# Two RWKV layers in a hybrid model's kernel: inverses by masked copies and transposes, the end by token halves, the first layer's mixing ahead of the norm

## The reference

```python
def rwkv7_time_mix(h, v_first, mix, w_rkv, ...):
    shifted = jnp.pad(h, ((0, 0), (1, 0), (0, 0)))[:, :-1]
    xm = h[:, :, None, :] + (shifted - h)[:, :, None, :] * mix
    r, k, v = einsum(xm[:, :, :3], w_rkv)
    logw = -softplus(-(w0 + tanh(xw @ w1) @ w2)) - 0.5      # decay
    a = sigmoid(a0 + (xa @ a1) @ a2)                        # rate
    g = sigmoid(xg @ g1) @ g2                               # gate
    # second RWKV layer: v = v + (v_first - v) * sigmoid(v0 + (xv @ v1) @ v2)
    def step(state, inp):
        sa = einsum('bhvk,bhk->bhv', state, kk_t)
        state = state * w_t - sa * (kk_t * a_t) + v_t * k_t
        return state, einsum('bhvk,bhk->bhv', state, r_t)
    y = (y - mu) * rsqrt(var + eps) * ln_w + ln_b           # per head
    y = y + sum(r * k * r_k) * v
    return (y * g) @ w_out
```

## Time and profile before

| what | value |
|---|---|
| median of 3 runs | 1935.93 us (1933.72 to 1939.68) |
| the profiled execution | 1935.0 us, its span 1932.9 us |
| TensorE matmuls busy | 1817.4 us (94%) |
| VectorE busy | 1263.3 us (65%) |
| ScalarE busy | 1029.7 us (53%) |
| GpSimd busy | 146.0 us (8%) |
| mean granted clock of TensorE | 0.974 |

### The profile page before, as it was taken

One profiled execution on the slowest core, in us unless ns is written; L12 is line 12 of the kernel. 1 busy time (PEld: TensorE's weight loads), 2 busy tenths in 40 slices (PEclk: granted clock), 3 DMA queues, 4 the chain that ended last, 5 costly groups with the idle time before them and its releaser, 6 DMA issues.

```text
span 1932.9 us, 43768 instructions
## 1 busy us (share of the span) xinstructions
PE 1817.4 (94%) x18871; PEld 1631.5 (84%) x18871; DVE 1263.3 (65%) x1783; ACT 1029.7 (53%) x1585; POOL 146.0 (8%) x106
## 2 busy tenths in 40 slices
PE   6987999999989999898999999998899999998998
PEld 5887788889979888887698888887798888887887
DVE  6875367865436675486668856876467755775764
ACT  5834455554535554354655545744465554564455
POOL 0051100000000000014000000151100000000000
PEclk9999999999989999899899999999999999998999
DMA  6420145557576655355465562320245555443441
GB/s 190 132 86 4 53 146 184 190 182 244 174 233 217 197 191 180 110 174 178 150 198 184 186 204 93 120 76 4 68 153 191 178 188 169 134 146 104 152 132 66
DMA packets 288535, 287.92 MB, mean 149 GB/s; under 512 B 15240, under 2 KB 286456, under 8 KB 288344
## 3 DMA queue, kind: packets, MB, share of 16 engines
q1 hardware_dynamic: 285048, 284.02, 45.8%
q10 hardware_dynamic: 3296, 1.11, 0.3%
HBM read 284.06 MB, written 1.05 MB: 148 GB/s over the span
## 4 chain that ended last, share of the span: by engine, by line
PE 90%; DVE 4%; issue 3%; ACT 2%; DMA 0%; POOL 0%; SPq 0%; DVEq 0%; ACTq 0%; POOLq 0%
PE ps L419 23%; PE ps L420 12%; PE ps L401 10%; PE ps L403 9%; PE ps L402 9%; PE ps L814 3%; PE ps L436 2%; PE ps L437 2%; PE ps L438 2%; PE ps L713 1%; PE ps L784 1%; PE ps L798 1%; PE ps L675 1%; PE ps L641 1%; PE ps L727 1%
## 5 line engine op out<-in xcount | busy, mean ns | idle before, releaser
L463 DVE TENSOR_TENSOR wl<-raw,wh 128x1024 fp32r<-128x1024 f32 x484 | 596.5, 1251 | 345.4 <-ACT wh L453 340.9
L453 ACT ACTIVATE wh<-raw 128x1024 fp32r<-128x1024 f32 x484 | 499.4, 1041 | 432.0 <-PE ps L420 191.2
L419 PE MATMUL ps<-HH,wh 128*128 128x512 f32 x1408 | 489.7, 391 | 0.0
L420 PE MATMUL ps<-HH,wl 128*128 128x256 f32 x1408 | 397.0, 282 | 0.0
L419 PEld LDWEIGHTS ps<-HH,wh 128*128 128x128 f32 x1408 | 264.3, 188 | 55.6 <-issue 0.4
L401 PE MATMUL ps<-HH,wh 128*128 128x256 f32 x928 | 271.4, 292 | 10.2 <-DVE HH L2498 5.5
L420 PEld LDWEIGHTS ps<-HH,wl 128*128 128x128 f32 x1408 | 266.1, 189 | 0.1
L402 PE MATMUL ps<-HH,wh 128*128 128x256 f32 x928 | 263.6, 284 | 0.0
L403 PE MATMUL ps<-HH,wl 128*128 128x256 f32 x928 | 263.3, 284 | 0.0
L401 PEld LDWEIGHTS ps<-HH,wh 128*128 128x128 f32 x928 | 179.3, 193 | 20.8 <-issue 6.6
L402 PEld LDWEIGHTS ps<-HH,wh 128*128 128x128 f32 x928 | 179.6, 193 | 1.2 <-issue 1.2
(11 more groups left out here) (323 smaller groups left out, 3119.6 us busy)
## 6 DMA issues: line engine op xcount, KB each, us to landing
raw<-in_ffn_w_gu_dram SPq DMA_DIRECT2D x88, 1024.0 KB, 5.1
raw<-in_ffn_w_down_dram SPq DMA_DIRECT2D x32, 1024.0 KB, 5.1
raw<-in_w_in_dram SPq DMA_DIRECT2D x32, 1024.0 KB, 5.4
raw<-in_rw_w_rkv_dram SPq DMA_DIRECT2D x24, 1024.0 KB, 5.3
B<-in_w_ada_dram SPq DMA_DIRECT2D x24, 1024.0 KB, 7.7
raw<-in_ds_w_in_dram SPq DMA_DIRECT2D x14, 1024.0 KB, 5.3
raw<-in_ffn_w_down_dram SPq DMA_DIRECT2D x16, 768.0 KB, 4.4
raw<-in_sb_w_qkv_dram SPq DMA_DIRECT2D x12, 1024.0 KB, 5.5
```

The costliest lines, as they stand in the source:

```text
L419: e.matmul(o[:, m, :], h_[:, k, c], x_, start=k0 + k == 0, stop=False, skip_group_check=True)
L420: i = e.matmul(o[:, m, 0:S], l_[:, k, c], x_[:, 0, :], start=False, stop=k0 + k == kt - 1, skip_group_check=True)
L453: e.activation(wh[:, u % UNITS, 0:kn * 256], raw[:, j % RAW, k0 * 256:(k0 + kn) * 256], ACT.Copy).then_inc(*up("hi"))
L463: e.tensor_tensor(wl[:, u % UNITS, 0:kn * 256], raw[:, j % RAW, k0 * 256:(k0 + kn) * 256], wh[:, u % UNITS, 0:kn * 256].bitcast(F32), ALU. ...
```

## The change

The inverse `T` starts as minus the identity (`clear`), and each level writes its off-diagonal quarter into it with `copy_predicated` under a mask `low{m}` (VectorE). The transpose of T comes no longer from a second product but from 16 transposes on TensorE a level (`turned`), copied by ScalarE. The left factor of a first product is the whole copy `At` of the gram, with no mask by level, so GpSimd's masks and the gram "bq" go. The projection blocks within the levels are split in two halves (`block_halves`) on a kept bank 0, the other tiles turn over seven banks. The grams "br" and "kr" and bTM's transposes move ahead of the product G. The end works by halves of 128 tokens: `centred(t)`, `spread(t, m)`, `weighted`, `gated`, `rest_y`; the gate multiplies before the scale, and gates 0 and 1 run earlier. In layer 0 the low-rank weights of decay and rate are mixed ahead of the normed input, with a semaphore of its own for the gate's weights; the mixing of the receptance's input moves behind the running sums, on ScalarE behind the first evacuation. The core of the diff:

```diff
+            for name, a, z, landed_ in (("rw_w1", 0, 64, s_down), ("rw_a1", 64, 128, s_down), ("rw_g1", 128, 256, s_down_g)):
+                e.dma_start(down[:, :, a:z], wview(A[name][n])[:, :, 0:z - a]).then_inc(landed_, 16)
...
+            def block_halves(m, p, g):
+                key, free = ("full", n, m, g), ("dve", ("vmix", n, g)) if n and m == 2 else ("act", ("full", n, m, g))
+                ready = [[("dve", ("xml", n, m, k // 2))] for k in range(KD)] if g == 0 else None
+                o = kept_bank(e, 0, key, free)
+                for k0, kn, u in next_units(KD):
+                    fm_unit(e, key, o, KD, k0, kn, u, parts_of(*((HH, HL), (XH, XL))[p]), ready)
+                    yield
...
+            def quarters(key, m, j, L, Rr, by):
+                os = [bank(e, (key, n, m, j, a), (by, (key, n, m, j, a))) for a in range(2)]
+                for q in range(8):
                     for b in range(2):
-                        for o, g in zip(os, pair):
-                            a = b ^ side_in(g) ^ side_out(g)
-                            i = e.matmul(o[half(b), p_ * HD:p_ * HD + HD], L[half(a), g[0], g[1], p_, :], Rr[half(a), g[0], g[1], p_, :],
+                        for a in range(2):
+                            i = e.matmul(os[a][half(b), q * HD:q * HD + HD], L[half(a), j, q, b, :], Rr[half(a), j, q, b, :],
                                          start=True, stop=True, skip_group_check=True)
-                            if p_ == 7 and b == 1:
...
+                            if q == 7 and b == 1:
+                                i.then_inc(*up("mm", (key, n, m, j, a)))
+            def turned(m, j):
+                for r in range(2):
+                    o = bank(e, ("turn", n, m, j, r), ("act", ("turn", n, m, j, r)))
+                    for q in range(4):
+                        i = e.transpose(o[:, q * P:q * P + P], BUF[6][:, (8 * j + 4 * r + q) * P:(8 * j + 4 * r + q) * P + P], ident)
+                    i.then_inc(*up("mm", ("turn", n, m, j, r)))
             def first_products(m):
-                for pair in pairs_at(m):
...
+                for j in range(2):
+                    for a in range(2):
+                        e.wait_ge(*at("act", ("bp", n, j, a)))
+                        e.wait_ge(*at("dve", ("low", n, m // 2, j, a)))
+                    quarters("xs", m, j, At, T, "dve" if m == 32 else "act")
+                for j in range(2):
+                    turned(m // 2, j)
             def second_products(m):
-                def s_in(g):
...
+                for j in range(2):
+                    for a in range(2):
+                        e.wait_ge(*at("dve" if m == 32 else "act", ("xs", n, m, j, a)))
+                        e.wait_ge(*at("act", ("turn", n, m // 2, j, a)))
+                    if m == 32:
+                        quarters("tt", m, j, Xw, Tw, "act")
+                    else:
+                        quarters("low", m, j, Tw, X1, "dve")
...
+            cur["first"] = 1
             for j in range(2):
                 gram("pb", j, Pm, Bt_)
             for j in range(2):
                 gram("bp", j, Bt_, Pm)
-            gram("bq", 1, Bt_, Pm, 1)
-            full(0, 1, 3)
-            first_products(2)
+            last_read = block_halves(0, 1, 3)
+            next(last_read)
...
+            next(last_read)
             for g in range(4):
-                full(2, 0, g)
+                first_products(LEVELS[g])
+                values = block_halves(2, 0, g)
+                next(values)
                 second_products(LEVELS[g])
-                if g < 3:
-                    first_products(LEVELS[g + 1])
+                next(values)
+            first_products(32)
             for j in range(2):
                 gram("kp", j, Kp, Pm)
+            second_products(32)
+            cur["first"] = 0
             for j in range(2):
                 pe_to_tm(e, ("pTM", n, j), Pm, j)
+            for j in range(2):
+                gram("br", j, Bt_, R_)
             e.wait_ge(*at("dve" if n else "act", ("vmix", n, 3) if n else ("full", n, 2, 3)))
             for j in range(2):
                 pe_to_tm(e, ("V", n, j), v_, j)
-            first_products(32)
             for j in range(2):
-                gram("br", j, Bt_, R_)
-            second_products(32)
+                gram("kr", j, Kp, R_)
+            for j in range(2):
+                pe_to_tm(e, ("bTM", n, j), Bt_, j)
             for j, par in groups:
                 e.wait_ge(*at("act", ("V", n, j, 1)))
...
+            def centred(t):
+                for m in range(2):
+                    if t == 0 and m == 1:
+                        cur["bank"] += 2
+                    o = bank(e, ("cen", n, t, m), ("dve", ("cen", n, t, 2 * m + 1)))
+                    e.wait_ge(*at("act", ("y", n, 2 * t + 1)))
+                    e.matmul(o[:, :], C("cent"), Y[:, 4 * m:4 * m + 4, t * P:t * P + P], start=True, stop=True,
+                             skip_group_check=True).then_inc(*up("mm", ("cen", n, t, m)))
+            def spread(t, m):
+                o = bank(e, ("var", n, t, m), ("act", ("var", n, t, m)))
+                e.wait_ge(*at("act", ("ysq", n, t, m)))
+                e.matmul(o[:, :], C("bavg"), ysq[:, 4 * m:4 * m + 4, :], start=True, stop=True,
+                         skip_group_check=True).then_inc(*up("mm", ("var", n, t, m)))
             own_values(0)
             keys_values(0, 2)
             y_values(0)
             from_state(1)
             new_state(1)
             new_y(1)
+            gate(0)
+            gate(1)
             keys_values(1, 1)
             y_values(1)
             from_state(2)
             new_state(2)
             new_y(2)
-            gate(0)
-            gate(1)
+            centred(0)
             from_state(3)
+            spread(0, 0)
+            spread(0, 1)
+            new_y(3)
             gate(2)
-            new_y(3)
+            centred(1)
+            spread(1, 0)
+            spread(1, 1)
+            cur["bank"] += 1
             gate(3)
-            Y, sq = FM(6), FM(0)
...
             pe_out_proj(e, layer, parts_of(XH, XL), [[("dve", ("yl", n, k // 2))] for k in range(KD)])
...
-            hi(e, 2 if n else 4)
-            prepare(1, HH)
+            hi(e)
+            if n:
+                prepare(1, HH)
             e.wait_ge(*at("mm", ("wa", n)))
             e.activation(lor[0:64, :], PS("wa", n)[0:64, 0:S], ACT.Tanh)
             e.activation(lor[64:128, :], PS("wa", n)[64:128, 0:S], ACT.Copy).then_inc(*up("act", ("wa", n)))
-            prepare(0, XH)
+            if n:
+                prepare(0, XH)
+            else:
+                prepare(1, HH)
+                hi(e)
             e.wait_ge(*at("mm", ("g", n)))
             e.activation(sg[:, 0, :], PS("g", n)[:, 0:S], ACT.Sigmoid).then_inc(*up("act", ("g", n)))
             for g in range(4):
...
+            if n == 0:
+                prepare(0, XH)
+                hi(e)
...
+            def clear(j):
+                e.wait_ge(*at("dve", ("rn read", n, j)))
+                e.activation(BUF[6][:, j * 1024:j * 1024 + 1024].rearrange("p (q t) -> p q t", t=HD),
+                             C("eye").unsqueeze(1).to_broadcast([P, 16, HD]), ACT.Copy, scale=-1.0).then_inc(*up("act", ("minus eye", n, j)))
             hi(e)
             evac(0, 0, R_)
             hi(e)
             evac(0, 1, R_)
+            clear(0)
+            clear(1)
             e.wait_ge(*at("mm", ("gv", n)))
             e.activation(sg[0:32, 1, :], PS("gv", n)[0:32, 0:S], ACT.Sigmoid).then_inc(*up("act", ("gv", n)))
...
+            def quarters_out(key, m, j, dst, scale=1.0):
+                for a in range(2):
+                    e.wait_ge(*at("mm", (key, n, m, j, 1)))
+                    e.activation(dst[:, j, :, a, :], q8(PS(key, n, m, j, a)[:, :]), ACT.Copy, scale=scale).then_inc(*up("act", (key, n, m, j, a)))
+            def turned(m):
+                for j in range(2):
+                    for r in range(2):
+                        copy_out(("turn", n, m, j, r), Tt[:, j, r, :])
             for j, par in groups:
...
+            e.wait_ge(*at("mm", ("gv", n)))
+            e.wait_ge(*at("dve", ("PB", n, 1)))
+            e.activation(BUF[0][:, :].rearrange("p (q t) -> p q t", t=HD), C("eye").unsqueeze(1).to_broadcast([P, 32, HD]),
+                         ACT.Copy).then_inc(*up("act", ("eye", n)))
+            evac(0, 3, R_)
             for g in range(4):
+                for j in range(2):
+                    quarters_out("xs", LEVELS[g], j, X1)
+                hi(e, 1)
+                turned(LEVELS[g] // 2)
                 hi(e, 1)
                 if n == 0:
                     evac(2, g, v_)
-                second_products(LEVELS[g])
...
             log_and_exp(e)
+            turned(16)
+            for j in range(2):
+                quarters_out("tt", 32, j, Tn, -1.0)
...
             negate_u(0)
             y_out(0)
             negate_u(1)
```

(123 more changed lines are left out.)

257 lines of the change are left out of this document (79 added, 178 removed).

## The result

The changed kernel takes 1941.95 us, median of 12 runs (1935.78 to 1948.90), against 1934.01 us of the kernel before in the same session (12 runs, 1930.53 to 1939.68). The ratio is 1.0039, 95% interval 1.0027 to 1.0051: it is slower by 0.4%. The prediction said 1921.0, in 1906 to 1940, and is wrong in sign and in range. The profiled execution took 1944.42 us, its span is 1942.3 (before: 1935.0 and 1932.9).

What follows compares the result with a forecast made beforehand. TensorE's work and waits in the two RWKV layers were taken as the bound; 1.9 + 13.3 + 1.5 + 7.4 - 6.8 - 3.4 = 13.9 us off 1935.0 gave 1921, range 1906 to 1940.

Steps and rivals of the forecast that it cites:

- list of the new kernel's waits: TensorE's work plus expected waits from gram to V transposes: 82.2 us in layer 0, 92.4 in layer 3.
- Opening, 1.9 us: Layer 0's start: TensorE begins 5.5 us earlier, ScalarE's list takes the rest, 1.9 us gained.
- Layer 0's inverses, 13.3 less 3.4 for two falls: Layer 0, gram to V: fewer waits, 95.5 to 82.2 us, 13.3 gained; two clock falls at 1.7 each taken off.
- a level of 14.25: One level of the inverses: 12.0 us of TensorE work plus a 2.25 us wait for ScalarE, without a clock fall.
- idle or slow: Layer 0's inverses before the change: 23.3 of 95.5 us in which TensorE was idle or at a lowered clock.
- Layer 3, 1.5 less 3.4 for two falls: Layer 3's inverses: 93.95 to 92.4 us, 1.5 gained; two clock falls at 1.7 each taken off.
- "waits change their name" rival: Opening and inverses: new waits eat the whole 13.9 us gain, 0.7 a level from ScalarE-VectorE turns; 1935 us, chance 0.11.
- Four of eight: Inverse levels of both layers: the 2.25 us wait makes the clock fall in four of eight, 1.7 us each, 6.8 lost.
- "fall in every level" rival: Clock falls in all eight inverse levels and at both ends, leaving 7.1 us gained; 1928 us, chance 0.17.
- Ends, 7.4 less 3.4: Ends of both layers: output projection's second unit 3.7 us earlier each, 7.4 gained; two clock falls, 3.4, taken off.
- The slower rival: VectorE's masked copies in the inverses cost from 1.2 us each; at 2.0 they give 1952 us; chance 0.12.

Runs made afterwards that it cites:

- e4: The kernel before with only the new opening of layer 0: 1934.1 us, ratio 0.9997 to the kernel before.
- e11: e7 with half a read block between the grams, constant products before the first key norm, masked copies before the value mix, erase-key turning between grams kp: 1891.6 us.
- e9: The changed kernel with 8 extra constant products on TensorE ahead of the wait in each lower level: 1928.8 us, ratio 0.9978 to the kernel before.
- e12: e7 with the weight piece that lands during the grams fetched only when the grams bp are done, both layers: 1899.6 us, ratio 0.9819 to the kernel before.
- e13: The kernel before with the weight piece that lands during the grams fetched only when the grams bp are done: 1931.8 us, ratio 0.9988.
- e1: The changed kernel with ScalarE copying the transposed banks before rounding the weight unit in each lower level: 1923.2 us, ratio 0.9937 to the kernel before.
- e6: e1 with VectorE subtracting a weight unit behind the level's masked copies instead of ahead of the decays: 1911.6 us, ratio 0.9872 to the kernel before.
- e7: e6 with ScalarE's identity copy and read-outs moved earlier and layer 3's value gates behind the last read block: 1906.8 us, ratio 0.9846 to the kernel before.
- e3: The kernel before with only the new layer ends by token halves: 1929.4 us, ratio 0.9973 to the kernel before.
- e2: The kernel before with only the new inverses, old opening and old ends: 1950.9 us, ratio 1.0090 to the kernel before.

## Why the prediction was wrong, step by step

Set beside the traces, the sum fails in two places. Up to layer 0's recurrence it had 1.9 + 13.3 - 3.4 = 11.8 us gained, and 0.6 were lost. For layer 3 it had 1.5 - 3.4, so 1.9 lost, and between layer 0's end and layer 3's recurrence 18.7 were lost. The ends, with all that follows layer 3's recurrence, gained 4.4 + 5.5 = 9.9 where 4.0 were forecast. The step that failed in both places is the list of the new kernel's waits, 82.2 us from the gram to the V transposes in layer 0 and 92.4 in layer 3. The traces have 96.0 and 109.8.

**Opening, 1.9 us: the times held, the gain did not.** Key norms ended at 64.89; predicted 64.9. But the prediction moved TensorE's start by 5.5 us and its key norm by 2 without pricing the idle time that this leaves ahead of the norm. TensorE was busy for 1.1 us of 58 to 61, the clock fell to 0.50, and the read block behind ran at 0.21 us a product instead of 0.12. The gain was gone by the gram; e4 measures 0.6 us, not to be told from zero. In e11, without the fall, the gram starts at 88.64, 1.4 us ahead of the predicted one.

**Layer 0's inverses, 13.3 less 3.4 for two falls: 82.2 us were 96.0.** Much of the mechanism was right: the rounding starts at the end of the half block, two copies behind it, 2.25 us; a level of 14.25 is 14.5 in e9. Also right: the masked copy at 0.72 us (predicted 0.69) and the subtraction at 1.2 without GpSimd, here in layer 3 (count, busy us and mean ns of one, idle before):

```profile
L456 DVE TENSOR_TENSOR wl<-raw,wh 128x1024 fp32r<-128x1024 f32 x14 | 16.9, 1221 | 50.4 <-ACT wh L446 50.4
L2330 DVE COPY_PREDICATED B<-CT,ps 128x512 f32<-128x512 int32 x20 | 13.1, 717 | 0.5 <-PE ps L812 0.5
```

The error is in the other side of the subtraction. Of the old kernel's 95.5 us the 23.3 "idle or slow" (23.5, if the list of TensorE's work is added up right, to 72.0) went in as recoverable unless a listed wait of the new kernel took their place. 2.45 of them was the unnamed stretch with 1.7 of fall behind it. The new list of waits did not hold it, and it stayed with 2.59 us; e12 and e13 show that all but 1 us of it in this layer hangs on the place of a weight transfer that both kernels have. The V transposes ended at 187.6 for the predicted 172.3: 5.8 us late at the first level (1.5 from the opening, the stretch, its fall), 5.8 more over the levels, most of it the falls (3.4 had been set down for them apart), and 3.7 in the tail, where two more unnamed stretches stand (1.23 and 1.35 us).

**Layer 3, 1.5 less 3.4 for two falls: 92.4 us were 109.8.** TensorE reached the first level at 1267.1, where the prediction's list, counted from the gram at 1245.8 (4.0 + 0.85 + 5.8 + 3.65), comes to 1260.1. These 7.0 us are the stretch of 2.79, not in the list, and the clock behind it (0.71 over 1252 to 1255, 0.50 over 1261 to 1264): both half blocks ran at up to 0.21 us a product, and the value gates took 4.49 us for 16 products (3.65 before). ScalarE's sigmoids, identity and evacuation then cost no more than the 4.0 that the list had for them. The levels took 7.4 more than forecast: 16.7 us each (roundings at 1277.69 and 1294.39) against 14.25 + 0.5, and of these 2 us a level 1.5 are the fall, since e9, without it, has 15.2. The rest fits VectorE's subtraction, which waits for a rounding, holds the value mixes, and these hold the kept bank. The last 3.0 us lie in the tail. e1 and e6, which change ScalarE's and VectorE's order alone, take 21 us of layer 3 back, waits and falls together, so that order was the cause of most of the loss. The "waits change their name" rival named the turns of ScalarE and VectorE, at 0.7 us a level; it named neither the stretch nor the falls.

**The clock: price right, count wrong.** 1.7 us a fall is confirmed by e9. Four of eight was a choice between 1.86 us (no fall) and 2.45 (fall); seven fell. The "fall in every level" rival was near in this count, not in its time (1928). The Trainium skill, "TensorE: Matmul & The Clock Gate", Part 4 (PE-mode transpose), says that the full clock does not engage for transposes. By it all eight would have fallen, one more than did, but the runs do not bear it out as the cause: e9 and e7 have the same 16 transposes a level, and their clock stays at 1.00 in all of layer 0's levels.

**Ends, 7.4 less 3.4: right within the noise.** The rounding behind the second unit, which started at 253.98, starts at 250.23:

```profile
250.23 1.06 ACT L446 ACTIVATE wh<-raw 128x1024 fp32r<-128x1024 f32 x1 [0.61 <-PE ps L391]
```

That is 46.5 us after the recurrence's first product, against 50.9 before (253.98 less 203.11, same instruction): 4.4 in layer 0. The fall forecast for this place came, inside that time:

```profile
243.00:245.00 2.00, 2.00 (x11) 0.50 1.09 378
```

So the trace has 4.4 where 3.7 less 1.7 was forecast. e3 measures 5.2 for both layers (3.1 to 7.3), which holds the forecast 4.0 and not twice 4.4; where the rest went, no run shows. The prediction's reading that TensorE had nothing to do from 240 to 246.70 before the change was not quite right: the windows from 243 to 247 have 1.75 us of work, at a clock of 0.83 and 0.50.

**The slower rival** came nearest with its sign, by the wrong mechanism: it needed masked copies of over 1.2 us, and they take 0.72. That the kernel came out slower, as this rival said, is luck.

## What to carry to other kernels

When an edit removes waits, list every idle stretch of the old kernel with its cause, and credit only those whose cause the edit removes; a stretch without a name stays until a run shows otherwise. In front of a busy TensorE, place on every helper engine first what TensorE waits for next and only then what it needs levels later: two such exchanges were worth 1.7% here. Price a wait with the clock fall behind it (1.7 us here, beside a wait of 2.25), and before moving a block ask what it covered.

## What the runs showed of the hardware

Eight useless products in each wait of 2.25 us make the kernel 0.61% faster, because the granted clock no longer falls (e9). After 163 to 227 records of 64 x 64 products in the grams TensorE pauses without a named cause: in layer 0 for 0.95 to 1.08 us where no weights move (e12, e13) and for 2.05 to 3.60 us where a 1 MB weight piece moves just ahead of the pause or beside it (ten traces, e3 to e2). In layer 3 the new order shows the same (1.00 in e12, 2.51 in e7), the old one does not (1.70 in e13, 1.04 to 1.86 with the transfer). VectorE's masked copy of 128 x 512 float32 from PSUM under an integer mask takes 0.72 us, the same as a plain product of that size to 0.03 us.
